# Two mixers on one Trainium2 core: another order of the steps from the gated norm to the long convolutions and in the merge

## What is computed

```
q, v, logf, k = projections of n                   # a gated linear recurrence, 4 heads of 128
o = recurrence in both directions                  # "oacc1"
o = rms_norm(o) * a_norm_w                         # over the 128 channels of a head
o_a = o * silu(n @ w_g)                            # the gates "g1s", one weight tile per head
v, x1, x2 = short_conv(n @ w_hy)                   # three taps, three times 4 groups of 128 channels
z = v
for order, gate in enumerate((x1, x2)):            # "hyena"
    z = gate * (fft_conv(z, kern[order]) + bias[order] * z)
y = sigmoid(g_a) * (o_a @ w_pa) + sigmoid(g_b) * (z @ w_pb)   # the merge, g_a and g_b are 16 tiles
out = y @ w_out
```

## Time and profile before

| what | value |
|---|---|
| median of 3 runs | 3578.05 us (3571.58 to 3578.14) |
| profiled execution, its own time | 3567.87 us |
| its span | 3565.9 us |
| instructions in it | 48983 |
| TensorE busy | 93% of the span |
| VectorE busy | 56% |
| ScalarE busy | 32% |
| granted TensorE clock, mean | 0.97 |
| DMA over the span | 95 GB/s |

### The profile page before, as it was taken

The page is one execution under the profiler, slowest core; times in us unless marked ns, Lnnn a source line. Parts: engine busy times, 40 slices in busy tenths (PEclk is TensorE's granted clock), DMA queues, the critical chain, the costliest instruction groups (busy, mean ns, idle before and its releaser), DMA issues.

```text
span 3565.9 us, 48983 instructions
## 1 busy us (share of the span) xinstructions
PE 3306.7 (93%) x18356; PEld 2872.8 (81%) x18356; DVE 1990.6 (56%) x2989; ACT 1145.1 (32%) x1588; POOL 131.6 (4%) x64
## 2 busy tenths in 40 slices
PE   6899999999998999999898879999999988789998
PEld 3599999978787877888677757999999766568887
DVE  6556443448856657884567574654433467653334
ACT  2221211245541123223443263311212343543223
POOL 3000000000000000000011100000000111100000
PEclk9799999999999999999999899999999999999999
DMA  5234332321122234553220111233322211113332
GB/s 214 99 118 141 118 130 83 118 93 38 36 94 64 78 118 171 189 194 112 67 78 25 36 42 62 104 130 126 130 90 73 79 40 38 48 50 105 94 94 94
DMA packets 101989, 339.95 MB, mean 95 GB/s; under 512 B 10351, under 2 KB 21487, under 8 KB 100432
## 3 DMA queue, kind: packets, MB, share of 16 engines
q1 hardware_dynamic: 82888, 301.91, 25.4%
q10 hardware_dynamic: 18952, 36.01, 2.9%
HBM read 323.73 MB, written 14.16 MB: 95 GB/s over the span
## 4 chain that ended last, share of the span: by engine, by line
PE 76%; DVE 13%; ACT 5%; issue 3%; DMA 2%; ACTq 1%; POOL 0%; SPq 0%; DVEq 0%; POOLq 0%
PE ps L425 61%; PE ps L467 3%; PE ps L451 2%; PE ps L1033 2%; ACT pr L2293 1%; DVE u_P L1188 1%; DMA hyena_k<-fst 1%; DVE u_ex L1144 1%; PE ps L1722 1%; DVE wr_lo L528 1%; DVE u_Z L1171 1%; PE ps L1709 1%; PE ps L1050 1%; ACT pT L2300 1%; ACT wr_hi L518 1%
## 5 line engine op out<-in xcount | busy, mean ns | idle before, releaser
L518 ACT ACTIVATE wr_hi<-raw 128x1024 fp32r<-128x1024 f32 x388 | 411.7, 1061 | 600.1 <-PE ps L425 543.5
L528 DVE TENSOR_TENSOR wr_lo<-raw,wr_hi 128x1024 fp32r<-128x1024 f32 x348 | 426.3, 1225 | 99.5 <-ACT wr_hi L518 68.5
L425 PE MATMUL ps<-xx_hi,wr_hi 128*128 128x512 f32 x1056 | 418.0, 396 | 0.7 <-ACT ff_gate L843 0.6
L425 PE MATMUL ps<-xx_lo,wr_hi 128*128 128x512 f32 x1056 | 413.8, 392 | 0.0
L425 PE MATMUL ps<-xx_hi,wr_lo 128*128 128x512 f32 x1056 | 413.8, 392 | 0.0
L891 DVE TENSOR_TENSOR ff_raw<-ps,ff_gate 128x768 f32<-128x768 f32 (+1 forms) x88 | 72.6, 825 | 576.7 <-PE ps L425 572.3
L425 PE MATMUL ps<-xa_hi,wr_hi 128*128 128x384 f32 x1344 | 341.1, 334 | 0.0
L425 PE MATMUL ps<-xa_hi,wr_lo 128*128 128x384 f32 x1344 | 341.0, 334 | 0.0
L425 PE MATMUL ps<-xa_lo,wr_hi 128*128 128x384 f32 x1344 | 340.9, 334 | 0.0
L572 DVE CUSTOM_DVE_ANT_0 ps<-raw,cb 128x1024 f32<-128x1024 f32 x240 | 295.4, 1231 | 53.5 <-DMA raw<-in_mod_stream 39.0
L425 PE MATMUL ps<-hid_hi,wr_hi 128*128 128x384 f32 (+1 forms) x1056 | 316.2, 353 | 3.8 <-DVE H L952 2.1
(11 more groups left out here) (402 smaller groups left out, 5190.2 us busy)
## 6 DMA issues: line engine op xcount, KB each, us to landing
raw<-in_stream SPq DMA_DIRECT2D x392, 512.0 KB, 3.6
raw<-in_mod_stream SPq DMA_DIRECT2D x168, 512.0 KB, 4.4
hK<-hyena_k ACTq DMA_DIRECT2D x4, 1152.0 KB, 6.0
h_kept<-H ACTq DMA_DIRECT2D x2, 2048.0 KB, 9.1
hyena_k<-fst ACTq DMA_DIRECT2D x14, 256.0 KB, 8.7
H<-in_h ACTq DMA_DIRECT2D x1, 3072.0 KB, 9.9
h_kept<-H ACTq DMA_DIRECT2D x1, 3072.0 KB, 10.1
H<-h_kept ACTq DMA_DIRECT2D x1, 3072.0 KB, 9.9
```

Source lines behind the costliest of these rows:

```text
L425: last = pe.matmul(gslot(slot)[:, col:col + n], w, rhs[part], start=(bi == 0 and pi == 0), stop=(bi == len(blocks) - 1 and pi == 2))
L518: act.activation(wr_hi[:, s, :], raw[:, s % RAW, :], ACT.Copy).then_inc(tile_hi, 1)
L528: dve.tensor_tensor(wr_lo[:, s, :], raw[:, s % RAW, :], wr_hi[:, s, :], ALU.subtract).then_inc(tile_lo, 1)
```

## The change

It has three parts. (A) In the passage TensorE's order becomes: gate tile 1, sums, tile 2, spreads 1 and 2, tile 3, spreads 3 and 4, tile 4. VectorE makes short convolutions 0 and 1 of group 0 and the fold first, then multiplies the recurrence's output by weight and spread in place, and each head by its gate when that gate is there (semaphore `gated`); the gate of the last head and the last two low halves come behind the copy of the first transposes (`finish`). ScalarE makes a head's high copy behind the next head's Silu. (B) In the convolutions, of the tile behind the inverse transform only 6 steps stay there; the other 2 come between the next transposes and their transform. The last tile stays whole. VectorE makes the low half of a weight tile behind the short convolutions and not ahead of them. (C) In the merge the last matmul of the first group counts on a new semaphore (`merge_half`), and VectorE takes the first product at that point.

```diff
--- before.py
+++ after.py
@@ -364,6 +364,7 @@
         dft_landed = semaphore("dft_landed")
         k_landed = semaphore("k_landed")
         hv_ready = semaphore("hv_ready")
+        gated, merge_half = semaphore("gated"), semaphore("merge_half")
         z_done = semaphore("z_done")
         freq_ready = semaphore("freq_ready")
         yraw_ready = semaphore("yraw_ready")
@@ -405,7 +406,7 @@
         def tile_slot(tally):
             return tally.n.get("tile_used", 0) % RING
-        def pe_tile(pe, tally, groups, order=None):
+        def pe_tile(pe, tally, groups, order=None, half_done=None):
 
@@ -425,6 +426,8 @@
                             last = pe.matmul(gslot(slot)[:, col:col + n], w, rhs[part],
                                              start=(bi == 0 and pi == 0),
                                              stop=(bi == len(blocks) - 1 and pi == 2))
+                if half_done is not None and gi == 0:
+                    last.then_inc(half_done, 1)
             last.then_inc(tile_used, 1)
             tally.passed("tile_used")
@@ -1546,11 +1549,28 @@
                 ktok_ready = pe_unit(pe, tally, unit(u1, u, 4), q1[:, h, :], k1[u % 2][:, :],
                                      lambda c, h=h: vtok1[:, c, h * P:(h + 1) * P], 1, NX, ktok_ready, ahead, head)
             pe_x_tiles(pe, tally, 1, False)
-            pe_head_norm(pe, tally, 4, NX, 1, ones[:, 0:2], hsq1, lambda: pe_x_tiles(pe, tally, 3, False))
-
-        def act_gates(act, tally, heads):
-            for h in heads:
+            pe.wait_ge(nsq_ready, tally.next("nsq_ready", 4))
+            pe_token_sums(pe, tally, [(hsq1[:, h, :], NX) for h in range(4)], ones[:, 0:2])
+            pe_x_tiles(pe, tally, 1, False)
+            pe.wait_ge(inv_ready, tally.next("inv_ready"))
+            for pair in range(2):
+                for h in (2 * pair, 2 * pair + 1):
+                    pe_spread(pe, tally, h * NX // P, NX)
+                pe_x_tiles(pe, tally, 1, False)
+
+        def act_gates(act, tally):
+
+            def high(h):
+                act.wait_ge(gated, tally.next("gated"))
+                act.activation(oab[0][:, h, :], g1s[:, h, :], ACT.Copy).then_inc(ohi_ready, 1)
+                act.wait_ge(ohi_ready, tally.next("ohi_ready"))
+
+            tally.passed("misc_done", 4)
+            for h in range(4):
                 act_proj(act, tally, g1s[:, h, :], NX, ACT.Silu)
+                if h:
+                    high(h - 1)
+            high(3)
         def act_forget(act, tally, u):
@@ -1610,8 +1630,13 @@
             act.wait_ge(misc_free[tally.place("misc_done", 1)], tally.read("misc_done"))
             act.dma_start(dft[:, :, :], ins["dft_fold"]).then_inc(dft_landed, 16)
             act.dma_start(idft[:, :, :], ins["idft_fold"]).then_inc(dft_landed, 16)
-            act_head_norm(act, tally, 4, NX, P, hsq1, oacc1, g1s, oab, 0,
-                          lambda: act.preload_act_table_set(LOG_EXP), lambda: act_gates(act, tally, range(4)))
+            act.wait_ge(misc_free[tally.place("misc_done", 1)], tally.read("misc_done"))
+            for h in range(4):
+                act.activation(hsq1[:, h, :], oacc1[:, h, :], ACT.Square).then_inc(nsq_ready, 1)
+                act.wait_ge(nsq_ready, tally.next("nsq_ready"))
+            act.preload_act_table_set(LOG_EXP)
+            act_inverse(act, tally, inv[:, 0:8 * NX // P], 8 * NX // P, P, (inv_ready, "inv_ready"))
+            act_gates(act, tally)
         def dve_forget(dve, tally, u):
@@ -1677,14 +1702,51 @@
             for _ in range(2):
                 dve_low_tile(dve, tally)
-            def gates_ready():
-                skip_tiles(tally, 4)
-                for _ in range(4):
-                    dve_low_tile(dve, tally)
-                for back in (1, 2):
-                    dve.wait_ge(slot_free[tally.place("group", back)], tally.read("group", back))
-
-            dve_head_norm(dve, tally, 4, NX, oacc1, g1s, vec("hgrn_w"), oab, 0, gates_ready)
+            tally.take("misc_done")
+            for back in (1, 2):
+                dve.wait_ge(slot_free[tally.place("group", back)], tally.read("group", back))
+            dve_conv1(dve, tally, 0, 0, (dve_step, "dve_step"))
+            dve_fold(dve, tally, hvs[0][:, 0, :])
+            dve_conv1(dve, tally, 0, 1, (dve_step, "dve_step"))
+            skip_tiles(tally, 4)
+            landed_gate = [(slot_free[tally.place("group", 4 - h)], tally.read("group", 4 - h)) for h in range(4)]
+
+            def spread(h):
+                ms = tally.take("misc_done")
+                dve.wait_ge(misc_done, tally.now("misc_done"))
+                dve.scalar_tensor_tensor(out=oacc1[:, h, :], in0=oacc1[:, h, :], scalar=vec("hgrn_w"),
+                                         in1=mslot(ms)[:, 0:NX], op0=ALU.mult, op1=ALU.mult).then_inc(misc_free[ms], 1)
+                dve.wait_ge(misc_free[ms], tally.read("misc_done"))
+
+            def gate(h):
+                dve.wait_ge(*landed_gate[h])
+                dve.tensor_tensor(g1s[:, h, :], g1s[:, h, :], oacc1[:, h, :], ALU.mult).then_inc(gated, 1)
+                dve.wait_ge(gated, tally.next("gated"))
+
+            def low(h):
+                dve.wait_ge(ohi_ready, tally.next("ohi_ready"))
+                dve.tensor_tensor(oab[1][:, h, :], g1s[:, h, :], oab[0][:, h, :], ALU.subtract).then_inc(mix_ready, 1)
+                dve.wait_ge(mix_ready, tally.next("mix_ready"))
+
+            dve_low_tile(dve, tally)
+            spread(0)
+            spread(1)
+            gate(0)
+            dve_low_tile(dve, tally)
+            gate(1)
+            low(0)
+            spread(2)
+            spread(3)
+            gate(2)
+            dve_low_tile(dve, tally)
+            low(1)
+
+            def finish():
+                gate(3)
+                low(2)
+                low(3)
+
+            return finish
 
@@ -1701,7 +1763,11 @@
                                             ident[:, :])
                     last.then_inc(misc_done, 1)
                     tally.passed("misc_done")
-                    pe.wait_ge(misc_free[tally.place("misc_done", 1)], tally.read("misc_done"))
+                    hu_copied = misc_free[tally.place("misc_done", 1)], tally.read("misc_done")
+                    if g or o:
+                        for k in (6, 7):
+                            pe_x_step(pe, tally, k, False)
+                    pe.wait_ge(*hu_copied)
                     place = tally.place("misc_done")
                     pe.wait_ge(misc_free[place], tally.free("misc_done"))
                     m = mslot(place)
@@ -1723,7 +1789,8 @@
                                          start=(i in (0, IDFT_EVEN)), stop=(i in (IDFT_EVEN - 1, len(IDFT_STEPS) - 1)))
                     last.then_inc(misc_done, 1)
                     tally.passed("misc_done")
-                    pe_x_tiles(pe, tally, 1, False)
+                    for k in range(KC if g == 3 and o else 6):
+                        pe_x_step(pe, tally, k, False)
         def act_hyena(act, tally):
             for s in range(4):
@@ -1747,31 +1814,29 @@
                 act_proj(act, tally, gate_at(4 * g + 3), NX, ACT.Sigmoid)
             act.dma_start(hback[:, :, :], h_kept).then_inc(h_back, 16)
-        def dve_hyena(dve, tally):
-            def conv(g, j, done):
...
-            def fold(src):
...
-            conv(0, 0, (dve_step, "dve_step"))
-            fold(hvs[0][:, 0, :])
+        def dve_conv1(dve, tally, g, j, done):
...
+        def dve_fold(dve, tally, src):
...
+        def dve_hyena(dve, tally, finish):
             for g in range(4):
                 hv = hvs[g % 2]
                 skip_tiles(tally, 4)
@@ -1781,16 +1846,19 @@
                     dve.tensor_copy(hu[:, :, :], mslot(ms)[:, 0:NX].rearrange("p (t f) -> p t f", f=P)
                         ).then_inc(misc_free[ms], 1)
                     dve.wait_ge(misc_free[ms], tally.read("misc_done"))
-                    if g or o:
+                    if o == 0:
+                        if g:
+                            dve_conv1(dve, tally, g, 1, (dve_step, "dve_step"))
+                        else:
+                            finish()
+                        dve_conv1(dve, tally, g, 2, (conv_done, "conv_done"))
                         dve_low_tile(dve, tally)
-                    if o == 0:
-
-                        conv(g, 1, (dve_step, "dve_step"))
-                        conv(g, 2, (conv_done, "conv_done"))
                         dve.wait_ge(k_landed, 16 * (g + 1))
-                    elif g < 3:
-                        conv(g + 1, 0, (dve_step, "dve_step"))
-                        fold(hvs[(g + 1) % 2][:, 0, :])
+                    else:
+                        if g < 3:
+                            dve_conv1(dve, tally, g + 1, 0, (dve_step, "dve_step"))
+                            dve_fold(dve, tally, hvs[(g + 1) % 2][:, 0, :])
+                        dve_low_tile(dve, tally)
```

(50 more changed lines are left out.)

## The result

The changed kernel takes 3539.68 us in the median of 4 runs (3537.39 to 3550.05); the kernel before has 3574.91 (3571.58 to 3578.14). The ratio is 0.9907 with a 95% interval of 0.9884 to 0.9931, so 25 to 41 us faster; two later measurements gave 0.9907 (0.9893 to 0.9920) and 0.9912 (0.9895 to 0.9928). Forecast was a gain of 26.5, to 3551.5 with a range of 3541 to 3562, and faster with 0.95. The gain was put too low.

What follows compares the result with a forecast made beforehand. TensorE's standstills and slow clock in the stretch 1033 to 1301 were taken as the bound. Passage 9.8, convolutions 8.2 and merge 8.5 sum to 26.5, off the median 3578.05 giving 3551.5 us, range 3541 to 3562.

Steps and rivals of the forecast that it cites:

- the transfer: Passage: hK, issued after the last head's low half, lands 6.0 later and holds the first inverse, leaving a 3.4 standstill.
- The slow clock's price: First inverse: the standstill before it lowers the clock and costs 1.7, with 0 and 3.4 as ends.
- The two convolutions and the fold: Passage: VectorE's some 5.3 of work falls into its 9.44 us before 1045.74 waiting for a weight tile's split, costing nothing.
- one more change between kinds of matmul: Convolutions: each cycle has one more such change, bounded by some 0.05, so 0.4 in all.
- 20.02 of "work": Convolutions: a cycle of 20.79 less the 0.77 gap leaves 20.02 of work; seven cycles take 140.1, 8.6 to win.
- That margin: First convolutions of groups 1 to 3: VectorE's 11.5 against TensorE's 12.0 fits with 0.5 to spare.
- VectorE becomes the bound: Rival, convolutions: the 0.5 margin is used up, the total gain is 19, time 3559; chance 0.11.
- 192 matmuls in 43.84: Merge: without the gap its 8 tiles run like the 8 tiles behind them; gain 8.5.
- the first rival: Passage: the spectrum's transfer does not hold the first inverse, or the clock stays up; gain 28.2 to 31.7; chance 0.14.
- The starving stream: Rival, convolutions: later low halves delay weight loads onto the path, 46 lost in 8 cycles, 19.5 slower, 3597.6; chance 0.03.
- All cases but the last gain 18 or more: Whole kernel: every case except the starving weight stream gains at least 18; faster was given 0.95.
- the signs of being wrong: Inverse waiting for VectorE in later cycles; output projection less than 22 us earlier than 1300.95; changed lengths behind it.

Runs made afterwards that it cites:

- e7: Changed kernel with hK loaded for group 0 in four pieces and the first convolution's low half moved behind the products: median 3541.97 us, ratio to before 0.9908.
- e11: Changed kernel with hK loaded for group 0 in four pieces, the low half in its old place: median 3538.84 us, ratio to before 0.9909.
- e8: The changed kernel measured once more, without an edit: median 3540.90 us, ratio to the kernel before 0.9907.
- e10: The changed kernel measured a third time, without an edit: median 3542.78 us, ratio to the kernel before 0.9912.
- e2: Changed kernel with all 8 steps behind the inverse and none under the copy, VectorE's new order kept: 3546.99 us (one execution).
- e3: Changed kernel with one step under the copy and seven behind the inverse: 3553.12 us (one execution).
- e4: Changed kernel with the low half ahead of the short convolutions again in the first convolution of groups 1 to 3: 3550.54 us (one execution).
- e5: Changed kernel with the passage of TensorE, ScalarE and VectorE as before, parts B and C kept: 3547.14 us (one execution).

## Why the prediction was right or wrong, step by step

**A, 9.8 forecast, 8.9 measured.** The order and the path were right: the last gate tile ended 30.7 behind the start (forecast 30.9), hK was issued at 34.7 (34.9), and it did hold the inverse. (Between the two the chain has one copy and two subtractions, where the forecast counted two copies and one; the sum came out the same by luck.) Mis-sized was the transfer, 7.2 instead of 6.0 with up to 1.0 allowed for a weight load beside it, and so the standstill, 4.6 instead of 3.4. The slow clock's price, taken as 1.7 from the drop after the sums, was 5.60 - 3.91 = 1.69, and e7 and e11 show that it goes with the standstill. That it came out to the hundredth is luck: behind about the same standstill the inverse took 5.60 to 6.16 in the profiles of the other kernels, 5.86 twice in the changed kernel's (e8, e10). The clock fell as TensorE began again behind the standstill, and was back at 1.00 from 1081 on. The rule of the Trainium skill ("TensorE: Matmul & The Clock Gate", What's actually happening) that activity releases the throttle agrees with 0.57 in the row of 1077 to 1081. The two convolutions and the fold cost nothing: VectorE still waited 4.6 for the split behind them.

**B, 8.2 forecast, 10.2 measured, above the upper end of 8.6.** The failed step is the one that priced "one more change between kinds of matmul" at 0.05 a cycle. A change costs nothing to speak of; it is the restart behind a wait that costs, 0.27, and the fill takes it away: the transform went from 4.73 to 4.46. The 20.02 of "work" in a cycle held that restart; the cycle is 19.8. e2 and e3 show it. The rest held: six steps still cover the fold, the copy came just in time (low half 1106.91 to 1107.60, copy at 1107.76). The products ended at 1118.71, 0.3 ahead of the inverse's place at 1118.98, where 0.5 was forecast. That margin was used up: the inverse's first weight load waited 0.2 for them in each of the three cycles, and the inverse took 3.95 in place of 3.91, so any more work on VectorE there would have counted. The rival "VectorE becomes the bound" did not happen; e4 shows that it does with the low tile left in its place.

**C, 8.5 forecast, 9.2 measured, above its upper end of 8.7.** The mechanism was right. The size was taken from 192 matmuls in 43.84, which is 5.48 a tile, but that block begins with a restart; the steady tile is 5.44. About half of the 0.6 too little is the merge's own tiles, the other half the projection, which no longer begins with a restart and which the forecast took as unchanged. VectorE did all its work in a tile's time. ScalarE waited once, 3.3 us, for a weight tile that landed beside the transfer back of H; TensorE did not notice.

**The sum.** 26.5 against 28.3 in the trace, 0.79% of the kernel. The sum is nearer than its parts: A gave 0.9 less than forecast, B 2.0 and C 0.7 more. 28.3 also lies in the band of the first rival (28.2 to 31.7), and yet that rival is out, as the transfer did hold the inverse and the clock did fall; the surplus is B's and C's. The medians say 35 with an interval of 25 to 41, of which the stretch explains 28.3. The starving stream (0.03) did not happen; nothing waited on TensorE's side for a weight tile. "All cases but the last gain 18 or more" held. The range in absolute time took too little for the scatter between measurements, which goes downwards too. Of the signs of being wrong, two did not show; the third, a changed length behind the stretch, cannot be told from the scatter of 2221.0 to 2228.2 us that one and the same kernel shows there.

## What to carry to other kernels

Count a standstill of TensorE as its length, plus a fixed restart of about 0.27 us, plus a possible stretch at the lower clock, so cover it wholly or the fixed part stays; and when work is put under a wait, look at what the work's own end releases, since here the fill pays only together with the new order on VectorE. Read the length of a steady tile from the middle of a block, not from a block that starts behind a wait. A gain of 5 us in one stage of a 3.5 ms kernel can be seen in the stage and drown in the whole, because behind a later standstill the clock stays low for 10, 17 or 24 us from one execution to the next: judge such a step by its stretch, and say that the whole did not confirm it.

## What the runs showed of the hardware that I had not expected

- The restart has a fixed price: behind waits of 0.05, 0.08, 0.15 and 0.78 us alike the transform took 4.73 instead of 4.46, or the inverse 4.17 instead of 3.91. Where the wait ends and the restart begins hangs on modelled matmul ends; the growth of whole cycles (e3 against e2) does not.
- Three equal standstills of 2.22 us (e4) lowered the clock twice and once not: 5.86, 5.86 and 4.17 for the same inverse.
- The first hK transfer took 7.0 to 7.4 in every kernel that issues it whole in the new passage, where the kernel before, e5 with the old passage, and the later transfers have 6.0 to 6.2. A weight load beside it is not the cause; the cause is open.
- The same standstill of 4.6 to 4.9 us near 2850 is followed by about 10, 17 or 24 us at the lower clock, and in the changed kernel alone by 10 once and 17 twice.
